# A hybrid decoder layer: modulation products taken whole on four column strips of TensorE, and norms by a reciprocal root with one Newton step

## What is computed

```
mod = silu(c) @ W_ada + b_ada  -> shift1, scale1, gate1, shift2, scale2, gate2
h   = RMSNorm(x, g_pre1) * (1 + scale1) + shift1
q, k, v, g, B, C, xv = split(h @ W_in)
ret = per-head GroupNorm(retention(rotary(q), rotary(k), v)) * silu(g)     4 heads
y   = B * causal_conv3(C * xv)
m   = concat(ret, y) @ W_out
x   = x + gate1 * RMSNorm(m, g_post1)
h   = RMSNorm(x, g_pre2) * (1 + scale2) + shift2
f   = PEER(h)      top-16 of 128^2 experts in 8 heads, weights from tables U, V
x   = x + gate2 * RMSNorm(f, g_post2)
```

## Time and profile before

| what | value |
|---|---|
| median of 3 runs | 1762.86 us (1760.16 to 1763.15) |
| the profiled execution, its own time | 1764.12 us |
| its span, first to last instruction | 1762.3 us |
| busy: PE, DVE, ACT, POOL | 1729.2, 1097.6, 587.3, 1043.2 us |
| mean granted clock of TensorE | 0.993 |
| DMA | 385 MB, 219 GB/s |
| start until the first projection block is done | 55.2 us |
| dense w_in stage | 55.85 to 211.4 us |
| heads | 212.2 to 279.7 us |
| output projection, norms | 279.7 to 354.3 us |

### The profile page before, as it was taken

One profiled execution on the slowest core, in us unless ns is written; L12 is line 12 of the kernel. 1 busy time (PEld: TensorE's weight loads), 2 busy tenths in 40 slices (PEclk: granted clock), 3 DMA queues, 4 the chain that ended last, 5 costly groups with the idle time before them and its releaser, 6 DMA issues.

```text
span 1762.3 us, 31194 instructions
## 1 busy us (share of the span) xinstructions
PE 1729.2 (98%) x12708; PEld 1688.9 (96%) x12708; DVE 1097.6 (62%) x2208; ACT 587.3 (33%) x764; POOL 1043.2 (59%) x693
## 2 busy tenths in 40 slices
PE   7999999999999999999999999999999999999996
PEld 5999979699999999999999999999999999999996
DVE  6724686568577366667552221224888989888884
ACT  5222264333323333232232222223333333333332
POOL 0340100006777888888888888874677777767721
PEclk9999999999999999999999999999999999999997
DMA  8523399673566665766667666668999999999971
GB/s 328 195 97 144 99 374 311 224 233 82 109 128 145 127 145 110 151 127 140 143 132 153 138 134 145 133 139 332 360 368 377 378 346 369 368 368 372 377 293 49
DMA packets 192358, 385.18 MB, mean 219 GB/s; under 512 B 74376, under 2 KB 132104, under 8 KB 177368
## 3 DMA queue, kind: packets, MB, share of 16 engines
q1 hardware_dynamic: 111864, 306.56, 51.3%
q0 software_dynamic: 80352, 76.65, 20.2%
HBM read 318.44 MB, written 64.19 MB: 217 GB/s over the span
## 4 chain that ended last, share of the span: by engine, by line
PE 94%; DVE 5%; ACT 1%; issue 0%; DMA 0%; SPq 0%; DVEq 0%; ACTq 0%
PE ps L1711 42%; PE ps L1734 30%; PE ps L669 12%; PE ps L720 3%; PE ps L783 2%; PE ps L615 1%; PE ps L1685 1%; DVE wl L1153 1%; DVE rs L1182 1%; PE ps L807 1%; DVE tg L1372 0%; PE ps L750 0%; DVE first_low L1153 0%; PE ps L736 0%; DVE qp L2022 0%
## 5 line engine op out<-in xcount | busy, mean ns | idle before, releaser
L99 POOL DMA_INDIRECT gates_dram<-gate,where x384 | 643.0, 1675 | 266.3 <-issue 252.2
L1711 PE MATMUL ps<-hh,ul 128*128 128x260 f32 x2048 | 412.8, 283 | 0.0
L1711 PE MATMUL ps<-hl,uh 128*128 128x260 f32 x2048 | 412.8, 283 | 0.0
L1711 PE MATMUL ps<-hh,uh 128*128 128x260 f32 x2048 | 412.1, 283 | 0.0
L1905 DVE TENSOR_TENSOR ul<-us,uh 128x1024 fp32r<-128x1024 f32 x132 | 161.2, 1222 | 350.9 <-issue 291.3
L1734 PE MATMUL ps<-cl,uh 128*128 128x384 f32 (+1 forms) x1024 | 345.0, 337 | 1.6 <-issue 1.1
L1734 PE MATMUL ps<-ch,uh 128*128 128x384 f32 x1024 | 344.1, 336 | 0.0
L1734 PE MATMUL ps<-ch,ul 128*128 128x384 f32 x1024 | 344.1, 336 | 0.0
L1711 PEld LDWEIGHTS ps<-hl,uh 128*128 128x128 f32 x2048 | 315.7, 189 | 0.4 <-issue 0.4
L1711 PEld LDWEIGHTS ps<-hh,ul 128*128 128x128 f32 x2048 | 315.8, 188 | 0.0
L1711 PEld LDWEIGHTS ps<-hh,uh 128*128 128x128 f32 x2048 | 314.8, 188 | 0.0
(11 more groups left out here) (248 smaller groups left out, 2238.8 us busy)
## 6 DMA issues: line engine op xcount, KB each, us to landing
us<-utab SPq DMA_DIRECT2D x128, 512.0 KB
pairs<-vtab SPq DMA_DIRECT2D x62, 1024.0 KB
gates_dram<-blank SPq DMA_DIRECT2D x24, 1024.0 KB, 10.1
ahead_dram<-a SPq DMA_DIRECT2D x128, 192.0 KB
qp<-ahead_dram SPq DMA_DIRECT2D x32, 768.0 KB
gt<-gates_dram SPq DMA_DIRECT2D x32, 768.0 KB
wr<-w_ada SPq DMA_DIRECT2D x21, 1024.0 KB, 7.9
wr<-w_in SPq DMA_DIRECT2D x13, 1024.0 KB, 4.7
```

What stands on the lines that cost most here:

```text
L99: nc.gpsimd.indirect_dma_start(out=io["gates"].rearrange("g p c a t -> (g p c a t)").unsqueeze(1), out_offset=bass.IndirectOffsetOnAxis(ap ...
L1711: last = nc.tensor.matmul(out[:, half, :], w, r[:, k, half * TH:(half + 1) * TH], start=(k == 0 and q == 0), stop=(k == KD - 1 and q == 2))
```

## The change

All 24 modulation rows are whole float32. `cs` is padded with zeros to 32 columns per slice, and matmul k of a product uses the 32-column strip k mod 4 of the array and writes to the 32 partitions of PSUM that belong to it, so a product leaves four partial sums. `copy_rows` copies all 128 partitions, and `ada_turn` turns them with `pick_row`, which adds nine rows out of each of the four strips. silu(c) is read from `given`, which lies in the second half of `rows`. `cp`, `both`, `first_high` and `first_low` are gone, and so are the splits of the 18 rows. The w_in tile that was sixth in the order of loads is now third. `inverse_rms` takes a first reciprocal root r of the mean square a from ScalarE (into `guess`) and one Newton step on DVE, r * (1.5 - 0.5 * a * r * r), in three operations; `guess` and `trial` lie in slices of `mix` that are free then. The orders of ScalarE and DVE at the start are written anew, the clears go two by two behind loads 11 to 22 (w_in but for the last), and products and turns sit ahead of slices 1 to 4.

```diff
 ADA, WIN, WOUT, WQ = "ada", "in", "out", "q"
+STRIP = 32
+STRIPS = P // STRIP
...
-    order = [(ADA, at) for at in shift_and_scale[:5]] + [(WIN, 0)] + [(ADA, at) for at in shift_and_scale[5:]]
+    order = [(ADA, at) for at in shift_and_scale[:2]] + [(WIN, 0)] + [(ADA, at) for at in shift_and_scale[2:]]
...
+        guess, trial = mix[:, KD - 1, :], mix[:, KD - 2, :]
...
-        cs = sb(stack, "cs", [P, KD, 1 + NS])
-        cp = sb(stack, "cp", [P, KD, 2 * (1 + NS)], F32R)
-        rows = sb(stack, "rows", [2 * (1 + NS), 2, WC])
-        both = sb(stack, "both", [2 * (1 + NS), 1 + NS])
+        cs = sb(stack, "cs", [P, KD, STRIP])
+        rows = sb(stack, "rows", [P, 2, WC])
+        pick_row = sb(stack, "pick_row", [P, 1 + NS])
+        given = rows[:, 1, 0:KD * (1 + NS)].rearrange("p (k c) -> p k c", k=KD)
...
-        def is_split(row):
-            return row < ROWS_2 and row not in (0, 4)
...
-                if not is_split(n_rows - 1):
-                    continue
-                used.append((mod_mm, n_rows))
+                continue
...
-                c = n - len(order) + CLEARS
+                c = 2 * (n - ROWS_1 - 3)
                 if c == 0:
                     sp.wait_ge(blank_ok, 1)
-                if 0 <= c < CLEARS:
+                for c in range(c, c + 2) if 0 <= c < CLEARS else ():
...
-                    sp.wait_ge(wl_ok, FIRST_IN + 1)
+                    sp.wait_ge(mod_mm, 5)
...
-                out = ps[0:2 * (1 + NS), banks[n % len(banks)], 0:WC]
-                if is_split(n):
-                    hi, lo = parts()
-                    for k in range(KD):
-                        for w in (hi, lo):
-                            last = nc.tensor.matmul(out, cp[:, k, :], w[:, k, :],
-                                                    start=(k == 0 and w is hi), stop=(k == KD - 1 and w is lo))
-                else:
-                    w = raw_buffers[weights(n)]
-                    for k in range(KD):
-                        last = nc.tensor.matmul(out[0:1 + NS], cs[:, k, :], w[:, k, :],
-                                                start=(k == 0), stop=(k == KD - 1))
+                bank = banks[n % len(banks)]
+                w = raw_buffers[weights(n)]
+                for k in range(KD):
+                    strip = slice(k % STRIPS * STRIP, (k % STRIPS + 1) * STRIP)
+                    last = nc.tensor.matmul(ps[strip, bank, 0:WC], cs[:, k, :], w[:, k, :],
+                                            start=(k < STRIPS), stop=(k >= KD - STRIPS))
...
-                    if is_split(n):
-                        last = nc.tensor.matmul(turned, made_rows, both[:], start=True, stop=True)
-                    else:
-                        last = nc.tensor.transpose(turned, made_rows[0:1 + NS], ident[0:1 + NS, 0:1 + NS])
+                    last = nc.tensor.matmul(turned, made_rows, pick_row[:], start=True, stop=True)
...
-            pe.wait_ge(clo_ok, 1)
-            pe.wait_ge(both_ok, 1)
-            ada_product()
-            ada_turn()
-            ada_product()
+            pe.wait_ge(silu_c, 1)
+            pe.wait_ge(pick_row_ok, 1)
             for _ in range(3):
                 ada_product()
                 ada_turn()
+            ada_product()
 
             def modulation_ahead(k):
 
-                if k == 1:
-                    for _ in range(3):
-                        ada_product()
-                        ada_turn()
-                if k == 2:
+                if k in (1, 2):
+                    ada_turn()
+                    ada_product()
+                if k == 3:
+                    ada_product()
+                    ada_turn()
+                if k == 4:
+                    ada_product()
+                    ada_turn()
                     ada_turn()
 
...
-                nc.scalar.activation(rs[:], rs[:], ACT.Sqrt).then_inc(rt_ok, 1)
+                nc.scalar.activation(guess, rs[:], ACT.Abs_reciprocal_sqrt).then_inc(rt_ok, 1)
...
-            nc.scalar.activation(cs[:], cs[:], ACT.Silu).then_inc(silu_c, 1)
-            act.wait_ge(silu_c, 1)
-            nc.scalar.activation(cp[:, :, 0:1 + NS], cs[:], ACT.Copy).then_inc(chi_ok, 1)
+            act.wait_ge(pad_ok, 1)
+            nc.scalar.activation(cs[:, :, 0:1 + NS], given, ACT.Silu).then_inc(silu_c, 1)
             for n in range(KD // 2):
                 act.wait_ge(in_x[n], 16)
                 nc.scalar.activation(mix[:, 2 * n:2 * n + 2], x[:, 2 * n:2 * n + 2], ACT.Square)\
                     .then_inc(sq_ok, 1)
             root(1)
+            copy_rows(2)
             high(0)
-            copy_rows(1)
-            high(1)
-            high(2)
-            copy_rows(2)
-            high(FIRST_IN)
             act.wait_ge(in_misc, 16 * 5)
             high_samples(0)
+            high_prompt(0)
             copy_rows(1)
-            high_prompt(0)
-            high(4)
             high_prompt(1)
-            high(5)
             copy_rows(1)
-            high(6)
             high_samples(1)
+            copy_rows(1)
+            high_prompt(2)
+            high_prompt(3)
             copy_rows(2)
-            high_prompt(2)
             high_samples(2)
+            high_prompt(4)
             copy_rows(1)
-            for k in (3, 4, 5):
-                high_prompt(k)
+            high_prompt(5)
+            high(1)
             high_samples(3)
-            for k in (6, 7):
-                high_prompt(k)
+            high_prompt(6)
+            high_prompt(7)
 
...
+            nc.gpsimd.memset(cs[:], 0.0).then_inc(pad_ok, 1)
             nc.gpsimd.memset(blank[:], 0.0).then_inc(blank_ok, 1)
-            pool.wait_ge(mod_mm, 5)
+            pool.wait_ge(mod_mm, 4)
...
-                link(nc.vector.reciprocal(rs[:], rs[:]))
+                link(nc.vector.tensor_tensor(trial, guess, guess, ALU.mult))
+                link(nc.vector.scalar_tensor_tensor(trial, trial, -0.5, rs[:], ALU.mult, ALU.mult))
+                link(nc.vector.scalar_tensor_tensor(rs[:], trial, 1.5, guess, ALU.add, ALU.mult))
...
             inverse_rms(1)
-            for i in range(3):
-                low(i)
             dve.wait_ge(in_misc, 16 * 5)
             link(nc.vector.tensor_tensor(tsm[:], x[:, :, SEQ:T],
                                          rs[:, SEQ:T].unsqueeze(1).to_broadcast([P, KD, NS]), ALU.mult))
             mod_pair(0)
             scaled_row(0)
+            low(0)
             scaled_row(1)
-            low(FIRST_IN)
             low_samples(0)
             low_prompt(0)
-            low(4)
+            low_prompt(1)
             mod_pair(1)
-            low(5)
-            low(6)
             scaled_row(2)
-            low_prompt(1)
             scaled_row(3)
             low_samples(1)
             low_prompt(2)
+            low_prompt(3)
             mod_pair(2)
             scaled_row(4)
-            low_prompt(3)
             scaled_row(5)
             low_samples(2)
             low_prompt(4)
+            low_prompt(5)
             mod_pair(3)
             scaled_row(6)
-            low_prompt(5)
+            low(1)
             scaled_row(7)
             low_samples(3)
             low_prompt(6)
...
-            low(HEADS_AT)
...
-                low(HEADS_AT + 3 * hd + 1)
                 if hd:
                     variances(hd - 1)
                     normalized(hd - 1)
-                low(HEADS_AT + 3 * hd + 2)
-                if hd:
                     low_rows(hd - 1)
                 if hd == RH - 1:
                     centered(hd)
-                low(HEADS_AT + 3 * hd + 3)
+                    low(OUT_AT)
```

More of the change, by code:

```diff
@@ L301, in build @@
         hl = sb(packed, "hl", [P, KD, T], F32R, "right")
-        first = ExitStack()
-        first_high, first_low = (sb(first, name, [P, 2, KD, WC], F32R) for name in ("first_high", "first_low"))
-        first.close()
         qp = sb(outer, "qp", [P, 2 * PH, T])
@@ L396, in mixer_stage @@
         raw_buffers = [wr[:, n] for n in range(NSLOT)] + [as_weights(b[:]) for b in (vt, ext, tg, pr)]
-        high_buffers = [wh[:, n] for n in range(2)] + [io["first_high"][:, n] for n in range(2)]
-        low_buffers = [wl[:, n] for n in range(2)] + [io["first_low"][:, n] for n in range(2)]
-        split_buffer, split_before = (2, 3, 1, 0, 2, 3, 1), {4: 0, 5: 1, 6: 2, 7: 6, 8: 3}
         def raw_slot(n):
@@ L411, in load_before @@
             return n - NSLOT - EXTRA if n < 2 * NSLOT + EXTRA else n - NSLOT
-        def buffer_of(i):
-            return split_buffer[i] if i < len(split_buffer) else i % 2
         w_slot = [sem(f"w_slot{n}") for n in range(NSLOT + EXTRA)]
@@ L602, in parts @@
                 pe.wait_ge(wl_ok, i + 1)
-                return high_buffers[buffer_of(i)], low_buffers[buffer_of(i)]
+                return wh[:, i % 2], wl[:, i % 2]
             def ada_product():
@@ L900, in copy_rows @@
                     act.wait_ge(mod_mm, n + 1)
-                    some = slice(0, (2 if is_split(n) else 1) * (1 + NS))
```

(27 more changed lines are left out.)

31 lines of the change are left out of this document (12 added, 19 removed).

## The result

The changed kernel takes **1752.67 us** (median of 7 runs, 1747.68 to 1754.78) against 1762.86 (7 runs, 1760.16 to 1768.64): ratio 0.9936, interval 0.9918 to 0.9954, 10.2 us less. It lies in the range and 2.3 us from the forecast. Its profiled execution took 1748.9 us, with a span of 1747.1: 15.2 us less than the one of before, and near the fast end of its own runs.

The account below looks back on a forecast made before the run. It took TensorE, busy 98% of the span, as the bound, with DVE and ScalarE on the chain at the start and norms. Start -5.5, heads 0, norms -2.5 gave -8 us: median 1755 us, range 1738 to 1766.

Parts of the forecast that it names:

- its own sign: Sign against the forecast: it is wrong if a modulation product lasts under 1.5 or over 2.4 us.
- the first rival: All four strips overlap: product 0.95 us, start -11, heads -10.5, norms -2.5, with clock loss about -22.5, 1740 us; chance 0.35.
- The price of a product: Each whole float32 modulation product on TensorE takes 2.0 us, since only two records overlap.
- the estimate of 3.2: Estimate from the skill page: four column tiles give 3.2 times the rate of one, a product of 1.1 us.
- Heads: Heads stage: 12 products at 2.0 for 1.95 us, +0.6; stalling splits gone, -0.7; together 0 us.
- The start: Kernel start: dense projection work begins at 50.4 us and not 55.85, -5.5 us.
- The walk: Step-by-step timing of the start, from product 0 at 14.4 us to dense work at 50.4; may be off by 5.
- Second and third norm: Second and third norm: three short operations replace the reciprocal, 1.25 us less each, both on the chain, -2.5 us.
- The first norm: At the start: reciprocal of 3.41 us becomes three operations, 2.15 with waits, 1.25 less; bounds 1.0 and 1.5.
- The table load: Before the second norm's root, ScalarE's 1.28 us table load just fits behind the last copy; at worst a few tenths.
- The clears: 24 writes of 1 MB move to the w_in loads: 0, at worst a few us; delaying w_in had chance 0.05.
- Half clock: In the all-strips-overlap case: TensorE gaps of nearly 4 us behind late norms; one restart at half clock costs 1.5 to 3 us.

Follow-up runs that it names:

- e3: The changed kernel with each strip used for two matmuls in succession instead of in turn; median 1748.88 us, ratio 0.9917.
- e6: The changed kernel with ScalarE's copy of a modulation row ahead of its copy of the normalised head in each head; median 1752.61 us.
- e2: The changed kernel with a product's eight matmuls on two column strips (even and odd k) instead of four; one run, 1772.6 us.
- e5: The changed kernel with VectorE's low part of the second w_in tile behind the last two rows of the modulated input; median 1748.25 us, ratio 0.9917.
- e7: The changed kernel with matmuls whose result nobody reads put in TensorE's idle stretches; median 1746.65 us, ratio 0.9911.
- e11: The kernel before with only the clearing stores moved early, two a load, as in the changed kernel; median 1763.51 us, ratio 1.0012.

## Why the prediction was right

The number was nearly right, by errors that cancelled; that is luck. By its own sign (a product under 1.5 us) the forecast's mechanism is refuted, and the mechanism of the first rival, which had a chance of 0.35, is the true one.

- **The price of a product** (2.0 us) is the step that failed. It measures 1.00. The reason given, "the second half of matmul k must wait for the first half, and only matmul k+1's first half can run beside it", is what `e3` refutes: the strips work side by side, in turn or not. The Trainium skill ("TensorE: Matmul & The Clock Gate", Part 3, Packing small matmuls) gives 2.38 for three column tiles. Here two give 3.57 / 1.85 = 1.93 and four 3.57, so the estimate of 3.2 drawn from that page was the better guide. The same part of the Trainium skill says that matmuls start and end in program order, which the starts in `e3` do not fit.
- **Heads** (0) follow from that: -9.5 measured. The rival said -10.5 and allowed 0.1 to 0.4 us a head for other waits. New waits for ScalarE's copies of 0.54, 0.54 and 0.80 us took some 1.9; with the row copy first (`e6`) the heads gain 11.3.
- **The start** (-5.5) is -4.9 in one profile and -8.4 in the other. The walk had products of 2.0 and full clock. There are products of 1.0 and half clock from 20 to 27 or 30 us, where a product takes 1.98 and a slice 2.90. That the two nearly cancel is luck: with a product of 1.85 (`e2`) the start gained nothing. So the splits taken from VectorE did not bring the walk's 5.5 by themselves. The rival's -11 left the clock aside at the start and took VectorE's tail as fixed; the tail is 2.1 us too long through the split in front of slice k = 6 (`e5`).
- **Second and third norm** (-2.5): measured -2.5, and -2.5 when taken out alone. The first norm is hidden, not behind a w_ada tile alone, but behind the small loads that VectorE needs.
- **The table load** (0): done at 314.11, the root waits for VectorE until 314.29. Right.
- **The clears** (0) are right for w_in, and in the kernel before their new place brings nothing. In the changed kernel their place is worth 6 us, in the heads. That "the queue becomes free, so its 12 weight tiles come easily" stood in the prediction, without a price: with the clears late, the faster heads ask for tiles sooner than the clears let them through.
- **Half clock** was a term of the first rival only (+1.5). It is the largest part of why products of 1 us did not bring the rival's 22.5. It costs 1.5 us at the query projection and 2.2 or 3.5 at the first late tile, and in the first profile 1.6 more behind slice k = 6. With most of it gone (`e7`) the median is 1746.65, below the forecast's own range of 1750 to 1762.
- **The rest**: no step had the border wait, 1.6 and 6.0 us in the two profiles of the changed kernel where before it was 1.1. How long it was in the runs without a profile, and so how much of the way from the first profile's -15.2 to the median's -10.2 it explains, is not shown.

## What to carry to other kernels

A matmul that fills 32 columns or fewer of the array should not go alone: independent slices of one sum on four column strips, added by the matmul that turns them anyway, gave 3.57 times the rate in float32. When an operation gets faster, ask what its slowness had covered: here a queue of stores, the order of two copies, a late store 900 us on, and TensorE's clock. An engine relieved of work gains nothing where others set the pace: with the splits gone and products of 1.85 us, start and heads took as long as before, in the one run there is. Before a gain is booked from one profile, look for a stage whose length differs between two profiles of the same kernel.

## What the hardware showed beyond the forecast

Four float32 matmuls of 256 columns on four strips start 7 ns apart and take as long as one; on two strips the rate is half of that, and the order of the strips doesn't matter (1.00 or 1.02 us).

The length of an idle stretch alone did not decide TensorE's clock here. Before slice k = 6 TensorE was idle for 2.82 us in both profiles of the changed kernel; the clock went to 0.5 from 47.2 to 50.6 us in the first and stayed full in the second. In the kernel before, an idle stretch of 2.85 us had half clock from 20.7 to 27.5 us, and one of 2.86 us in `e11` none. The same kernel had half clock at the start until 26.6 us in one execution and until 30.1 in another. Matmuls that nobody reads kept the clock full where they stood, cost nothing that could be seen, and their kernel's median is 6 us lower.
